# Scaling the probabilities of two heads: two ScalarE operations or one VectorE operation

## The reference

```python
def sliding_window_attention(q, k, v, sinks):
    ...
    s = jnp.einsum('bnqkgd,bnskd->bnkgqs', qb, kb,
                   preferred_element_type=jnp.float32) * scale
    s = jnp.where(mask[None, :, None, None], s, -jnp.inf)
    m = jnp.maximum(jnp.max(s, axis=-1, keepdims=True), sink)
    p = jnp.exp(s - m)
    p = p / (jnp.sum(p, axis=-1, keepdims=True) + jnp.exp(sink - m))
    o = jnp.einsum('bnkgqs,bnskd->bnqkgd', p.astype(v.dtype), vb)
```

```python
        merged = jax.nn.sigmoid(ga) * a_out + jax.nn.sigmoid(gb) * c_out
        x = x + jnp.einsum('btd,de->bte', merged, w_out[l])
```

## Time and profile before

| | us |
|---|---|
| median of 3 runs (2263.87 to 2264.66) | 2263.9 |
| the profiled execution | 2265.19 |
| its span | 2263.3 |
| PE busy | 2236.3 (99%) |
| DVE busy | 1254.1 (55%) |
| ACT busy | 938.1 (41%) |
| POOL busy | 235.0 (10%) |

### The profile page before, as it was taken

The page is one execution under the profiler, slowest core; times in us unless marked ns, Lnnn a source line. Parts: engine busy times, 40 slices in busy tenths (PEclk is TensorE's granted clock), DMA queues, the critical chain, the costliest instruction groups (busy, mean ns, idle before and its releaser), DMA issues.

```text
span 2263.3 us, 29343 instructions
## 1 busy us (share of the span) xinstructions
PE 2236.3 (99%) x11388; PEld 1819.1 (80%) x11388; DVE 1254.1 (55%) x1842; ACT 938.1 (41%) x1507; POOL 235.0 (10%) x218
## 2 busy tenths in 40 slices
PE   9999999999999999999999999999999999999999
PEld 7887888898888888876778888888886668888887
DVE  6467656345444226998664444333989654544433
ACT  5545454354333234226954333222333963433322
POOL 3000032020000001022030000001003122000001
PEclk9999999999999999999999999999999999999999
DMA  5221033123222322221122222222321112322232
GB/s 215 105 75 57 20 131 131 38 75 112 93 93 93 112 94 95 85 93 44 51 75 94 98 106 93 93 104 93 112 75 56 48 66 75 130 93 93 93 112 74
DMA packets 29909, 203.20 MB, mean 90 GB/s; under 512 B 3440, under 2 KB 4080, under 8 KB 6128
## 3 DMA queue, kind: packets, MB, share of 16 engines
q1 hardware_dynamic: 28512, 197.34, 24.5%
q10 hardware_dynamic: 1296, 4.46, 0.5%
HBM read 199.69 MB, written 2.10 MB: 89 GB/s over the span
## 4 chain that ended last, share of the span: by engine, by line
PE 87%; DVE 8%; ACT 2%; issue 2%; POOL 1%; DMA 0%; ACTq 0%; POOLq 0%; DVEq 0%
PE bank L415 25%; PE bank L417 25%; PE bank L416 25%; DVE cy L2352 3%; PE bank L999 1%; PE bank L2130 1%; PE bank L2117 1%; PE bank L2107 1%; DVE w_lo L301 1%; PE bank L970 1%; POOL acc L324 1%; PE bank L987 1%; PE bank L2007 1%; PE bank L1590 1%; PE bank L1567 1%
## 5 line engine op out<-in xcount | busy, mean ns | idle before, releaser
L415 PE MATMUL bank<-x_hi,w_hi 128*128 128x512 f32 (+1 forms) x2032 | 790.0, 389 | 6.3 <-DVE w_lo L301 2.7
L417 PE MATMUL bank<-x_hi,w_lo 128*128 128x512 f32 (+1 forms) x2032 | 775.1, 381 | 0.0
L416 PE MATMUL bank<-x_lo,w_hi 128*128 128x512 f32 (+1 forms) x2032 | 774.1, 381 | 0.0
L301 DVE TENSOR_TENSOR w_lo<-w_raw,w_hi 128x2048 fp32r<-128x2048 f32 x167 | 386.5, 2315 | 404.9 <-ACT w_hi L297 404.9
L297 ACT ACTIVATE w_hi<-w_raw 128x2048 fp32r<-128x2048 f32 x167 | 319.7, 1916 | 586.7 <-PE bank L417 584.9
L415 PEld LDWEIGHTS bank<-x_hi,w_hi 128*128 128x128 f32 x2032 | 382.2, 188 | 84.7 <-issue 6.8
L417 PEld LDWEIGHTS bank<-x_hi,w_lo 128*128 128x128 f32 x2032 | 382.0, 188 | 74.6
L416 PEld LDWEIGHTS bank<-x_lo,w_hi 128*128 128x128 f32 x2032 | 382.5, 188 | 72.5 <-issue 2.9
L415 PE MATMUL bank<-f_hi,w_hi 128*128 128x512 f32 (+1 forms) x572 | 215.2, 376 | 0.0
L416 PE MATMUL bank<-f_lo,w_hi 128*128 128x512 f32 (+1 forms) x572 | 215.0, 376 | 0.0
L417 PE MATMUL bank<-f_hi,w_lo 128*128 128x512 f32 (+1 forms) x572 | 215.0, 376 | 0.0
(11 more groups left out here) (354 smaller groups left out, 2650.9 us busy)
## 6 DMA issues: line engine op xcount, KB each, us to landing
w_raw<-w_d SPq DMA_DIRECT2D x184, 1024.0 KB, 4.8
out_d<-h SPq DMA_DIRECT2D x4, 512.0 KB, 6.1
h<-x_d ACTq DMA_DIRECT2D x3, 512.0 KB, 9.2
tab<-rope_d ACTq DMA_DIRECT2D x2, 640.0 KB, 3.9
memT<-mem_d ACTq DMA_DIRECT2D x1, 1024.0 KB, 4.9
w_raw<-w_d SPq DMA_DIRECT2D x2, 256.0 KB, 4.2
h<-x_d ACTq DMA_DIRECT2D x2, 256.0 KB, 6.0
w_raw<-w_d SPq DMA_DIRECT2D x1, 512.0 KB, 6.5
```

What stands on the lines that cost most here:

```text
L301: dve.tensor_tensor(w_lo[:, u.slot, :], w_raw[:, u.slot, :], w_hi[:, u.slot, :], ALU.subtract).then_inc(lo_ready, 1)
L415: pe.matmul(dst, wh[:, k, cols], hi[:, kx_, at:at + width], start=start, stop=False)
L416: pe.matmul(dst, wh[:, k, cols], lo[:, kx_, at:at + width], start=False, stop=False)
L417: return pe.matmul(dst, wl[:, k, cols], hi[:, kx_, at:at + width], start=False, stop=stop)
```

## The change

ACT's two scalings per job, one for each head, with a copy by a scale, are gone. DVE multiplies both heads' probabilities in one `tensor_tensor` with the pair of reciprocals (broadcast along the keys), right behind the reciprocal of the same job; it first waits for its own reciprocal. `turn` counts one increment of the semaphore per job where it counted two.

```diff
@@ turn(j), on PE
-                pe.wait_ge(A["scaled"], (L * LJ + j) * 2 + 2)
+                pe.wait_ge(A["scaled"], L * LJ + j + 1)
@@ on ACT
-            def scaled(j):
-                c0 = P if block_of(j) == 0 else 0
-                act.wait_ge(A["rec"], L * LJ + j + 1)
-                act.wait_ge(A["exp"], (L * LJ + j) * 2 + 2)
-                for e in range(2):
-                    act.activation(lprob[:, prob_at(j), e, c0:2 * P], lprob[:, prob_at(j), e, c0:2 * P], ACT.Copy,
-                                   scale=asm(j, 12, e)).then_inc(A["scaled"], 1)
-
...
-                if 0 <= t - 1 < LJ:
-                    scaled(t - 1)
@@ softmax(j, o), on DVE
                     dve.reciprocal(asm(o, 12), asm(o, 4)).then_inc(A["rec"], 1)
+                    c0 = P if block_of(o) == 0 else 0
+                    row = lprob[:, prob_at(o), :, c0:2 * P]
+                    dve.wait_ge(A["rec"], L * LJ + o + 1)
+                    dve.tensor_tensor(row, row, asm(o, 12).unsqueeze(2).to_broadcast([P, 2, 2 * P - c0]), ALU.mult).then_inc(A["scaled"], 1)
```

## The result

| | kernel before | changed kernel |
|---|---|---|
| median of 6 runs, us | 2263.9 (2262.5 to 2264.7) | 2270.8 (2268.9 to 2273.3) |
| ratio | 1 | 1.003, 95% interval 1.0018 to 1.0042 |
| profiled execution / its span, us | 2265.19 / 2263.3 | 2269.07 / 2267.3 |

The changed kernel is slower by 6.9 us where 3.2 was forecast; 2270.8 lies 0.8 us above the range. The profiled execution is one of the two shortest of the six.

The account below looks back on a forecast made before the run. PE, busy for 99%, was taken as the bound, so only its waits count: 0.55 + 1.05 = 1.6 us per layer, 3.2 in all, giving a median of 2267.1 us; range (8 times in 10) 2263.0 to 2270.0.

Parts of the forecast that it names:

- DVE's multiply: Added on DVE, one per job: 0.70 us for 48 long jobs, 0.44 for 16 short ones, 41 us in all.
- meetings with POOL: Multiplies 3, 4 and 30 can each stand until an addition of POOL is over: 0.3 to 0.7 us.
- Place 1: Turns of jobs 2 and 3: DVE's late row mean delays ACT's copies; PE loses 0.93 us, then 0.35 more.
- Place 2: Turn of job 7: masks 2.3 us late, ACT spared two pairs of scalings; PE leaves at +0.55 us.
- Between jobs 8 and 28: PE waits for nobody; DVE's 0.7 us more per step is covered and costs nothing.
- Place 3: Step 31, first output product: last evacuation late by multiplies 29 and 30 and POOL's addition; 1.05 us, bounds 0.7 to 1.4.
- The sum: Both attention layers: 0.55 + 1.05 = 1.6 us per layer, 3.2 us in all.
- Rival 2: DVE becomes the bound at the start, its chain to job 7's masks over 3 us late: 2269.3 to 2271; chance 0.23.
- My signs: Wrong if PE's first turn waits don't grow, job 7's wait stays, or new waits appear between jobs 8 and 28.

Follow-up runs that it names:

- bridged kernel: Changed kernel with idle transposes on PE, 14 before the scores of job 5 and 13 before the first output product: 2266.6 us, ratio 1.0013.
- held copy: Kernel before, no multiply on DVE, with ACT computing the second square of step 3 three times, so its copy comes late: 2268.2 us, ratio 1.0019.

## Why the prediction was wrong, point by point

- **DVE's multiply, 0.70 and 0.44 us, 41 us in all: right.** 0.69 at 512 columns and 0.42 at 256 (two heads of 128), 43.0 in all; the meetings with POOL, taken as 0.3 to 0.7, are 0.65 at multiplies 3 and 4 and 0.2 at 30. One reading behind them was off: the long half of a split ended 1.08 us after POOL's addition (1053.66 against 1052.58), not 1.22; the excess of 0.7 us stands. ACT was to be less busy by 54 us and was so by 43.4.
- **Place 1: right.** The wait at job 2 was to grow by 0.93 and grew by 0.92 in the changed kernel (PE came to it 0.13 late as well); job 3 was to add 0.35, and the bridged kernel shows 0.38. With the first five multiplies back on ACT both go.
- **Place 2: right.** PE was to leave at +0.55; it leaves at +0.72 where no clock falls, by the path named: masks of job 7 2.35 us late, two pairs of scalings gone from ACT behind them. The gain from ACT is real, as the kernels with DVE on jobs 5 to 27 or 5 to 8 show from the other side (0.8 us per layer at the turn of job 7).
- **Between jobs 8 and 28: right.** No new wait, and twice the multiply needs 0.6 us.
- **Place 3: right, 0.97 for 1.05**, and by the path named: the evacuation ended 0.97 us later (1146.50 against 1145.53, at a place where the two executions are level) and the output product stood for it.
- **The sum, 3.2 us: right as the sum of the waits, wrong as the forecast of the time.** The bridged kernel's runs stand at +2.8, its trace, which has no fall in the attentions, at 2 x 1.69 = 3.4. The step that failed is the one that took "PE loses 0.93 us more", and at place 3 "1.05 us", for the whole cost of a longer wait: a fall of the clock was put at nothing, without a reason. In this kernel such a stand has a second cost in a part of the cases, a clock of 1.2 GHz for 3.4 us behind it, of which 1.1 us was left once place 2 was passed, and 1.5 at place 3. Four stands were lengthened (two per layer); 4.2 of the 6.9 us went when PE was kept at work in them.
- **Rival 2's number came closest (2269.3 to 2271), by another mechanism.** DVE's chain to the masks of job 7 was 2.35 us late and not over 3, and place 2 did give back 0.7 us; what made up the difference was the clock.
- **My signs.** That PE's waits would not grow, that job 7's wait would stay or that new waits would appear in the middle, would each have proved me wrong; none came true, and the time was outside all the same. The signs had nothing on PE's clock, though the granted clock stands in the same row as the busy times I read the earlier trace rows.

That lengthened stands bring falls of the clock, and that these cost the time which the waits don't, is shown by the bridged kernel and by the held copy; whether a given stand is followed by a fall is only a frequency. In the eleven profiled executions other than that of before, weight loads were 1.97 us or more apart 20 times in the two attentions, and the clock fell behind 14 of these (six of eight at 1.97 to 1.98 us, none of two at 2.27, seven of eight at 2.5, one of two at 2.9). It never fell behind the stands of 1.6 us that the kernel before has at job 2, nor behind those in the kernels that keep them (ten in all), nor behind the two of 1.87 us at job 0 of the kernel with the multiply at the end of the step. What decides within such a place stays open. The runs' own numbers agree with it: the changed kernel's two runs with a mean granted clock of 0.998 took 2268.9 and 2269.1, the one with 0.997 took 2270.3, the three with 0.996 took 2271.2 to 2273.3; the bridged kernel's stood at 0.998 to 1.0.

The Trainium skill ("TensorE: Matmul & The Clock Gate", Part 1) tells of such a gate between half and full rate, set by how busy PE has been; the windows above agree on the two levels (0.50 and 1.00).

## What to carry to other kernels

Where one engine is busy for 99%, price a wait that your change lengthens twice: once for itself, and once for the clock behind it, and look in the existing trace for stands of the new length and PEclk after them. Work moved off an engine pays only at the jobs in which that engine is waited for: here at jobs 5 to 8, while the same edit cost time at the first and the last jobs; so try it there alone (here that was worth 0.1% at most). And when work moves to DVE, ask for each of its new neighbours what POOL does at that moment.

## What the hardware showed that I had not expected

- Stands of PE of 2.0 to 2.9 us are followed, 14 times in 20, by 3.4 us of granted clock at 1.2 GHz; the changed kernel does it at the same place in one layer and not in the other. Falls also come at 224 us (3.4 or 6.8 us long, in the kernel before too) and at 317 us.
- A DVE operation with a broadcast operand from SBUF stands for POOL as one with two full operands does: 1.34 against 0.69 us. The fused one (`SCALAR_TENSOR_TENSOR` with both sources in SBUF) does too, 1.76 against 0.68 us. The Trainium skill ("SBUF — State Buffer", section "SBUF: two separate sides") says that the one that starts first keeps the port pair for its whole instruction. The rows of the multiply at the end of the step agree: POOL's began at 1142.72, DVE's at 1142.90, and it is DVE's that stood; in the changed kernel DVE's began first (1143.62 against 1143.78), took 0.68 us, and POOL's took 1.65 instead of 1.29.
- Removing 53.9 us of busy ACT instructions took 43.4 us off its busy time, since neighbours overlap: a pair reads 0.90 us, and the next operation begins 0.80 us after the pair began.
